# Expert rows gathered whole, against rows gathered as a first half and a second half by index, with part of the second halves left out

## The reference, cut to what matters

```python
u = jnp.take(expert_u, eidx, axis=0)
h = jax.nn.gelu(jnp.einsum('thkd,td->thk', u, xb))
vv = jnp.take(expert_v, eidx, axis=0)
return jnp.einsum('thk,thkd->td', (g * h.astype(jnp.float32)).astype(xb.dtype), vv)
```

## Time and profile before

| | |
|---|---|
| median of three runs | 3214.01 us |
| the three runs | 3214.01, 3211.82, 3215.86 us |
| profiled execution: span from the first to the last instruction | 3210.9 us |
| busy: PE, DVE, ACT, POOL | 79%, 49%, 33%, 18% |
| moved | 1067.8 MB, mean 333 GB/s |

### The profile page before, as it was taken

One profiled execution on the slowest core, in us unless ns is written; L12 is line 12 of the kernel. 1 busy time (PEld: TensorE's weight loads), 2 busy tenths in 40 slices (PEclk: granted clock), 3 DMA queues, 4 the chain that ended last, 5 costly groups with the idle time before them and its releaser, 6 DMA issues.

```text
span 3210.9 us, 43682 instructions
## 1 busy us (share of the span) xinstructions
PE 2530.9 (79%) x17242; PEld 1248.3 (39%) x17242; DVE 1564.1 (49%) x3391; ACT 1048.7 (33%) x2457; POOL 581.5 (18%) x535
## 2 busy tenths in 40 slices
PE   8999988797988878878879878897778655555655
PEld 6677774484322222222228634343324211111111
DVE  4655655763100100100107466678675777777764
ACT  2533443521000000000006354577344444343433
POOL 0000000000000000000000143344443444444442
PEclk9999998998999999999999989898888777788778
DMA  4211302249999999999995499999999999999997
GB/s 152 101 58 66 122 26 112 92 158 382 427 427 427 427 427 427 427 427 427 427 411 195 176 418 399 417 418 383 420 419 420 420 420 419 420 419 420 420 419 331
DMA packets 128670, 1067.80 MB, mean 333 GB/s; under 512 B 14289, under 2 KB 17233, under 8 KB 27601
## 3 DMA queue, kind: packets, MB, share of 16 engines
q0 software_dynamic: 75456, 543.20, 41.0%
q1 hardware_dynamic: 53008, 521.81, 39.4%
HBM read 1051.58 MB, written 13.37 MB: 332 GB/s over the span
## 4 chain that ended last, share of the span: by engine, by line
DMA 50%; PE 34%; DVE 7%; ACT 6%; issue 2%; POOL 1%; ACTq 0%; DVEq 0%; SPq 0%; POOLq 0%
PE ps L92 33%; DMA gb<-in_peer_uv,eidx 27%; DMA gw<-in_eu 14%; DMA gw<-in_ed 8%; DVE gb L146 2%; PE ps L97 2%; ACT L168 1%; ACT dots L168 1%; ACT diag L168 1%; ACT prob L168 1%; POOL gb L86 1%; DVE prob L146 0%; DVE w_lo L115 0%; ACT prob_t L168 0%; DVE prob L120 0%
## 5 line engine op out<-in xcount | busy, mean ns | idle before, releaser
L92 PE MATMUL ps<-gb,diag 64*64 64x512 f32 x4096 | 662.0, 759 | 410.3 <-ACT diag L168 396.8
L146 DVE CUSTOM_DVE_ANT_0 gb<-gb,xn 128x1024 f32<-128x1024 f32 x512 | 627.1, 1225 | 378.5 <-DMA gb<-in_peer_uv,eidx 378.0
L86 POOL DMA_INDIRECT gb<-in_peer_uv,eidx x512 | 570.3, 1114 | 1312.6 <-PE ps L92 718.5
L92 PEld LDWEIGHTS ps<-gb,diag 64*64 64x64 f32 x4096 | 148.2, 155 | 847.6 <-ACT diag L168 746.3
L168 ACT ACTIVATE dots<-dots 128x1 f32<-128x1 f32 (+1 forms) x382 | 77.6, 203 | 618.3 <-DVE dots L146 611.5
L115 DVE TENSOR_TENSOR expert_act<-expert_act,ps 128x512 f32<-128x512 f32 x32 | 22.0, 687 | 523.8 <-PE ps L92 523.2
L92 PE MATMUL ps<-ga,xt 128*64 128x512 f32 x1024 | 229.2, 596 | 41.3 <-DMA ga<-in_eu 32.6
L92 PE MATMUL ps<-gw,xt 128*64 128x512 f32 x992 | 224.3, 601 | 25.4 <-DMA gw<-in_eu 16.2
L168 ACT ACTIVATE diag<-cons,dots 128x128 f32<-128x128 f32 x512 | 205.5, 401 | 41.1 <-ACT dots L168 0.4
L115 DVE TENSOR_TENSOR x<-x,ps 128x512 f32<-128x512 f32 (+1 forms) x96 | 61.4, 643 | 296.5 <-PE ps L92 294.9
L168 ACT ACT_TABLE_LOAD x124 | 159.1, 1283 | 8.1 <-PEq L3241 0.7
(11 more groups left out here) (360 smaller groups left out, 3616.9 us busy)
## 6 DMA issues: line engine op xcount, KB each, us to landing
ga<-in_eu SPq DMA_DIRECT2D x47, 2048.0 KB, 35.5
gw<-in_eg SPq DMA_DIRECT2D x46, 2048.0 KB, 30.7
ring<-in_wt SPq DMA_DIRECT2D x75, 1024.0 KB, 6.0
gw<-in_ed SPq DMA_DIRECT2D x32, 2048.0 KB, 35.5
ga<-in_ed SPq DMA_DIRECT2D x32, 2048.0 KB, 36.1
ga<-in_eg SPq DMA_DIRECT2D x17, 2048.0 KB, 32.2
gw<-in_eu SPq DMA_DIRECT2D x16, 2048.0 KB, 35.5
p_scratch<-spill SPq DMA_DIRECT2D x35, 256.0 KB, 2.1
```

The source lines that it names most:

```text
L86: self.e.indirect_dma_start(out, None, table, bass.IndirectOffsetOnAxis(ap=idx, axis=0)).then_inc(s, 16)
L92: i = self.e.matmul(out, l, r, start=st, stop=sp, skip_group_check=True)
L146: self.done(self.e.tensor_tensor_reduce(out=o, in0=a, in1=b, scale=scale, scalar=start, op0=o0, op1=o1, accum_out=acc), name)
```

## The change

Two views of the same table are used: `peer_uv` as 16384 lines of 8 KB, and `halves`, 32768 lines of 4 KB, in which expert e has its u at 2e and its v at 2e + 1. In each group of four rows (a quad) the first one stays whole, except the first of each block; the other three are fetched in two steps: u at 2e, then, once the four dot products of the quad are there, v at 2e + 1. The index of v gets 65536 added in partitions where the dot product is at or below -11 (`NO_GELU`), where the gelu is exactly zero here; the gather of v has a limit of 32767 on its indices and leaves out those above it, whose partitions then keep what the buffer held, with a weight set to zero. Quads in which a v buffer is used for the first time fetch all of v. Rows 496 to 511 stay whole.

- POOL issues, for each quad g: the four u or whole rows of quad g + 1, then the v of quad g.
- DVE does three more operations of 128x4 for each quad (two `stt` and a `ts`), a doubled index in `dv_choose` in place of a copy, and one more operation on `eidx` a head.
- ACT takes the gelu once for four rows, after DVE's `mask`.
- Sums run up to eight rows behind the dot products. Each buffer of 2048 is used as a u half (free when the dot product is done) and a v half (free after the sum), or for whole rows: 5 pairs and 2 whole from the start, 7 and 3 from row 172, 9 and 4 from row 244.

```diff
+        at = bass.IndirectOffsetOnAxis(ap=idx, axis=0)
+        if last is None:
+            self.e.indirect_dma_start(out, None, table, at).then_inc(s, 16)
+        else:
+            self.e.indirect_dma_start(out, None, table, at, bounds_check=last, oob_is_err=False).then_inc(s, 16)
...
+    NO_GELU, FAR = -11.0, 65536.0
+    halves = I["peer_uv"].rearrange("e (t d) -> (e t) d", t=2)
...
+    def whole(n):
+
+        return n % 4 == 0 and n % 128 != 0 or n >= WHOLE
...
+    U_AT, u_last = places(SPLIT, U_PIECES, "dot")
+    V_AT, v_last = places(SPLIT, V_PIECES, "sum")
+    W_AT, w_last = places([n for n in range(WHOLE) if whole(n)], ROWS_OF, "sum")
...
+    def gated(g):
+
+        return g < WHOLE // 4 and not any(V_AT[n][2] for n in quad(4 * g) if not whole(n))
+
+    def sums_after(n):
+
+        g, j = n // 4, n % 4
...
+        out = []
+        if j == 0 and g >= 1 and whole(4 * g - 4):
+            out.append(4 * g - 4)
+        if j and g >= 2:
+            if j == 1 and not whole(4 * g - 8):
+                out.append(4 * g - 8)
+            out.append(4 * g - 8 + j)
+        return out
...
-            for m in group:
-                yield ("u", m)
-            yield ("w", group)
...
+            yield ("u", n)
+            if n % 4 == 3 or n >= LAST:
+                yield ("k", n)
+            for m in sums_after(n):
+                yield ("w", m)
...
+                pe.wait_ge(("diag", n))
+                if not whole(n):
+                    pe.wait_ge(("v_row", n))
...
+            elif ev[0] == "k":
                 n = ev[1]
...
+                ac.wait_ge(("mask", n // 4) if n < WHOLE else ("dot", n))
+                ac.act(d, d, ACT.Gelu_apprx_tanh, name=("gelu", n))
...
-        dv.cp(sif, siu)
+        dv.ts(sif, siu, 2.0, MUL)
...
+            elif ev[0] == "k" and ev[1] < WHOLE:
+                n = ev[1]
+                i, k = n // 128, n % 128 - 3
+                d, e = dots[:, i % 2, k:k + 4], eidx[i % 2][:, k:k + 4]
+                if gated(n // 4):
+                    s4 = soft[:, i % 2, k:k + 4]
+                    dv.wait_ge(("inv", i, k // 16))
+                    dv.ts(far, d, NO_GELU, ALU.is_le, FAR, MUL)
+                    dv.stt(e, far, 1.0, e, ADD, ADD, name=("v_idx", n // 4))
+                    dv.stt(s4, d, NO_GELU, s4, ALU.is_gt, MUL, name=("mask", n // 4))
+                else:
+                    dv.ts(e, e, 1.0, ADD, name=("v_idx", n // 4))
+                    dv.mark(("mask", n // 4))
...
+        def v_row(n):
+            i, k = n // 128, n % 128
+            s, freed, _ = V_AT[n]
+            po.wait_ge(("v_idx", n // 4))
             if freed is not None:
                 po.wait_ge(freed)
-            po.gather(buf_of(n), I["peer_uv"], eidx[i % 2][:, k:k + 1], f"gb{s}", ("row", n))
+            po.gather(v_of(n), halves, eidx[i % 2][:, k:k + 1], f"gv{s}", ("v_row", n), 2 * 16384 - 1 if gated(n // 4) else None)
+
+        for n in quad(0):
+            u_row(n)
+        for g in range(WHOLE // 4):
+            for n in quad(4 * g + 4):
+                u_row(n)
+            for n in quad(4 * g):
+                if not whole(n):
+                    v_row(n)
+        for n in range(WHOLE + 4, 512):
+            u_row(n)
```

More of the change, by code:

```diff
@@ new lines, in quad, with places @@
+    def quad(n):
+        return range(n - n % 4, n - n % 4 + 4)
+    def places(rows, pieces, end):
+        held, out = [None] * len(pieces), {}
+        for n in rows:
+            s = min((held[s] is not None, rows.index(held[s]) if held[s] is not None else s, s)
+                    for s, (_, first, _) in enumerate(pieces) if n >= first)[2]
+            out[n] = (s, pieces[s][2] if held[s] is None else (end, held[s]), held[s] is None)
+            held[s] = n
+        return out, held
+    SPLIT = [n for n in range(512) if not whole(n)]
@@ L2786, in peer_order @@
+    SUMS = [m for n in range(512) for m in sums_after(n)]
+    assert sorted(SUMS) == list(range(512)) and all(a // 128 <= b // 128 for a, b in zip(SUMS, SUMS[1:]))
+    SUM_AT = {m: q for q, m in enumerate(SUMS)}
+    ROW_ENDS = [SUMS[127], SUMS[255], SUMS[383], LAST - 1]
+    assert SUMS[LAST - 1] == LAST - 1
     def peer_order():
@@ L2791, in peer_order @@
         pass_rows = [24 + 31 * k // 10 for k in range(-1, 52)]
-        n = 0
-        while n < 512:
-            group = row_group(n)
+        for n in range(512):
             ahead = 16 + min(8, n) + max(0, min(8, (n - 8) // 4))
-            need = min(32 * STEPS, STEPS * (ahead + group[-1]) // 16) if n > 2 else STEPS
+            need = min(32 * STEPS, STEPS * (ahead + n) // 16) if n > 2 else STEPS
             while done < need:
@@ L2827, in peer_order @@
                 yield ("q", 1, (n - 194) // 6)
-            n = group[-1] + 1
     def sp_peer(sp):
@@ L2884, in pe_peer @@
+                i, at = n // 128, SUM_AT[n]
+                v, dg = v_of(n), diag[at % 4]
+                if n >= LAST:
+                    if n == LAST:
+                        ends = [few.next() for _ in range(2)]
+                        pe.wait_ge(*ends[0][2], *ends[1][2])
                     pe.wait_ge(("diag", n))
-                    if k == 0:
-                        pe.wait_ge(*left if i == 0 else [("rows_end", i - 1)])
                     for half in range(2):
                         for r in range(2):
[L2889 to L2892, removed]
+                            q = slice(64 * r, 64 * r + 64)
+                            pe.mm(PS[ends[half][0]][q, :], dg[q, q], v[q, 512 * half:512 * half + 512],
+                                  n == LAST, n == 511, ("sum", n) if half and r else ("sum_half", n) if r else None)
+                    continue
@@ new lines, in pe_peer @@
+                pe.wait_ge(("diag", n))
+                if not whole(n):
+                    pe.wait_ge(("v_row", n))
+                if at % 128 == 0:
+                    pe.wait_ge(*left if i == 0 else [("rows_end", i - 1)])
+                for half in range(2):
+                    for r in range(2):
+                        to = r if half == 0 else 1 - r
+                        pe.mm(PS[VB[half]][64 * to:64 * to + 64, :], dg[64 * r:64 * r + 64, 64 * r:64 * r + 64],
+                              v[64 * r:64 * r + 64, 512 * half:512 * half + 512], at % 128 == 0, n == ROW_ENDS[i],
+                              ("sum", n) if half and r else None)
@@ L2937, in ac_peer @@
                     soft_of(ac, i, h)
-            elif ev[0] == "u":
+            elif ev[0] == "k":
                 n = ev[1]
[L2940 to L2945, removed]
-            elif ev[0] == "w":
[L2947 to L2954, removed]
+                first = n if n >= LAST else n - 3
+                i, k = first // 128, first % 128
+                d = dots[:, i % 2, k:k + n - first + 1]
+                ac.wait_ge(("mask", n // 4) if n < WHOLE else ("dot", n))
+                ac.act(d, d, ACT.Gelu_apprx_tanh, name=("gelu", n))
+            elif ev[0] == "w":
+                n = ev[1]
+                i, k, at = n // 128, n % 128, SUM_AT[n]
+                d = dots[:, i % 2, k:k + 1]
+                ac.wait_ge(("inv", i, k // 16))
+                if n < WHOLE:
+                    ac.wait_ge(("mask", n // 4))
+                ac.act(d, d, ACT.Copy, scale=soft[:, i % 2, k:k + 1], name=("weight", n))
+                if at >= 4:
+                    ac.wait_ge(("sum", SUMS[at - 4]))
+                ac.act(diag[at % 4], ident, ACT.Copy, scale=d, name=("diag", n))
             elif ev[0] == "out":
                 i = ev[1]
-                ac.wait_ge(("sum", min(128 * i + 127, LAST - 1)), ("dot", 128 * min(i, 2) + 127))
+                ac.wait_ge(("sum", ROW_ENDS[i]), ("dot", 128 * min(i, 2) + 127))
                 if i == 3:
@@ L3009, in dv_choose @@
         yield
-        dv.stt(eidx[i % 2][:, 16 * h:16 * h + 16], e12[:, 0, :], 128.0, e12[:, 1, :], MUL, ADD, name=("eidx", i, h))
+        dv.stt(eidx[i % 2][:, 16 * h:16 * h + 16], e12[:, 0, :], 128.0, e12[:, 1, :], MUL, ADD)
+        w_ = eidx[i % 2][:, 16 * h:16 * h + 16]
+        if (i, h) != (3, 7):
+            w_ = w_[:, 0 if h else 4:16:4]
+        was, dv.link = dv.link, None if dv.link is None else dv.n
+        dv.ts(w_, w_, 0.5, MUL, name=("eidx", i, h))
+        dv.link = was
         yield
@@ L3057, in po_peer, with u_row @@
     def po_peer(po):
-        for n in range(512):
+        def u_row(n):
             i, k = n // 128, n % 128
-            s, freed = ROW_SLOTS[n]
             po.wait_ge(("eidx", i, k // 16))
+            at = eidx[i % 2][:, k:k + 1]
+            if n >= WHOLE:
+                t, sem, freed = tail_at(n)
+                po.wait_ge(freed)
+                po.gather(t, I["peer_uv"], at, sem, ("row", n))
+            elif whole(n):
+                s, freed, _ = W_AT[n]
+                if freed is not None:
+                    po.wait_ge(freed)
+                po.gather(ROWS_OF[s][0], I["peer_uv"], at, f"gw{s}", ("row", n))
```

(12 more changed lines are left out.)

69 lines of the change are left out of this document (45 added, 24 removed).

## The result

Before 3214.18 us median of four runs, after 3379.91 us (3368.89 to 3386.21, four runs): a ratio of 1.0512, 95% interval 1.0489 to 1.0535. The change makes the kernel 5% slower, where 2.2% faster was forecast. The profiled execution took 3368.89 us with a span of 3367.1, 156.2 above the span of before; it is the fastest of the four, so what follows tells 156 us where the medians differ by 166.

The account below looks back on a forecast made before the run. POOL's gather issues were taken to become the limit in place of bytes: rows 0 to 243 -44, 244 to 495 -12, end -21, start +7, together -70 us. That gave 3140 us of span, 3143 us median; range 3060 to 3245.

Parts of the forecast that it names:

- the loop through POOL: Round from a quad's mask through v and u gathers back to it; 10.8 us a quad early, adding 34 us.
- rival 3: Early loop costs 12 us a quad, DMA engines idle while POOL waits for PE: 3195 us; chance 10%.
- about +65: Upper bound of the change in time, taken with the early loop at 12 us a quad; the fast bound was -174.
- rival 2: POOL's issues fall into step with DVE's dot products, 10.7 us a quad: 3243 us; chance 25%.
- What POOL pays: POOL issues 872 gathers instead of 496, at 1.425 us early and 1.39 late: 10.0 and 9.7 us a quad.
- the price of parity: Issues starting at random meet a running dot product in half the cases and wait 0.25 us on average.
- the late round: Late loop of v, u, dot products and mask takes 17.1 us for two quads, less than 2 x 9.7: hidden.
- The DMA floor: 158 half rows saved, 161 ns a packet; DMA work falls to about 1212 us, -174 if nothing else binds.
- rival 4: The index limit leaves nothing out, or a skipped pick costs as long as a copied one: 3240 us; chance 3%.
- Rival 1: DMA stays the limit, POOL's stalls shrink or limited gathers issue cheaply: 3040 to 3100 us; chance 17%.
- The -21: Gain at the end: sixteen whole rows and a short queue, 40 + 5.5 us where it was 40 + 26.6.
- DVE's added operations: Three small operations add 0.6 us a quad, 7.5 in all, beneath POOL's 9.7: free while POOL binds.

Follow-up runs that it names:

- six_v_pieces: The changed kernel with a fifth early u piece turned into a sixth v piece; 3296.94 us, ratio 1.0258.
- split_from_176: The changed kernel with rows 0 to 175 fetched whole and summed at once, two-step fetching from row 176; 3253.67 us, ratio 1.0114.
- from_176_lead: split_from_176 with, from quad 62 on, u of quad g + 2 issued ahead of v of g; 3241.69 us, ratio 1.0075.
- from_176_psum: split_from_176 with dot products from row 256 on reading the normed token from PSUM; 3195.83 us, ratio 0.9938.
- xn_in_psum: The changed kernel with dot products from row 256 on reading the normed token from PSUM; 3369.35 us, ratio 1.0478.
- no_limit: The changed kernel with every v fetched in all 128 partitions, no index limit and no mask; 3363.44 us, ratio 1.0461.
- psum alone: Only the token read from PSUM from row 256 on: 3369.35 us on the changed kernel, 3195.83 us on split_from_176.
- all_from_0_lead_psum: The changed kernel, split from row 0, with token in PSUM from row 256 and u two quads ahead from quad 62; 3279.61 us, ratio 1.0199.
- from_176_lead_psum: split_from_176 with both token in PSUM from row 256 and u two quads ahead from quad 62; 3154.96 us, ratio 0.9813.

## Why the prediction was wrong, point by point

**The step that failed is "the loop through POOL", and in it the early quads.** I took 10.8 us a quad, with 12 as the bad end; it was 14.6. That alone is 43 x 3.8 = 164 of the 227 us between 3140 and 3367. Its terms: landing was taken at 5.5, the shortest of 1816 to 2506 us, where the median was 14.1; by the updates of the gathers' semaphores in the trace of after it is, in the median, 7.6 for u and 6.4 for v in rows 0 to 171, 6.9 and 5.9 in rows 244 to 495. Dot product and mask were taken at 1.9, as if one row were late; four landed rows stand in line on DVE, with choosing steps between, 6.5 us (2920.0 to 2926.5 in the trace of after), though part of that passes while the last of them is still in flight. And the third v went out 14.3 us after the start of the last dot product, not 6.0: by the kernel's order the sum it waits for stands behind this quad's gelu and whatever PE and ACT have in hand of the mixing layer (how much each of them costs no run tells apart). Over quads 20 to 41 (those that meet the start of a block left out) the round has, in the mean, 13.7 us to the third v, 5.7 to the last u, 7.9 for its landing and 2.5 to the start of its dot product: 29.9 for two quads, where 18.6 was reckoned, 24 with all that might stand in its way. I had the mechanism (rival 3) and priced it as a sum of shortest durations, so its 12 wasn't a bound. six_v_pieces and split_from_176 show it. (Nor does the "about +65" of the sum follow from its own terms: rival 2 and the loop at 12 together are -70 + 100 + 52 = +82.)

**"What POOL pays" was right in kind, short in size.** POOL became the limit late (gaps of 0.30, from_176_lead), at 1.48 us an issue and not 1.39: 7 x 0.09 x 63 = 40 us, more than the 35 by which rows 244 to 495 missed. The mean that I took came from issues spread out by waits for PE; of those that follow one another at once, the kernel before already shows 1.43 us from 2506 to 3175 (60 of them) and 1.49 over the whole stage (174). The stall of the earlier trace rows ended 0.81 us after the dot product did, as all others; the forecast read 0.89, from the start of the record behind it. I had written that starts at random would meet a dot product in half the cases and called it "the price of parity". That is what happened: 197 of 392. Rival 2's in-step pattern wasn't needed. It said that it decides from 1.49.

**A second limit stood close behind it.** I called the late round hidden, 17.1 against 2 x 9.7. It holds 2 x 9.66 when the issues aren't held up (from_176_psum), longer than 17.1 for the two sizes named above, and loosening it takes the quads on to 8.98. In after POOL limits and the round is close: from_176_lead gains only 12 us. The 10 us of xn_in_psum it doesn't explain; see "Open".

**The DMA floor was right in its parts.** 158 half rows, 76,048 packets of 4 KB for the layer forecast as about 76,000, 159 ns for 161. The 9.0 us a quad was reached as 8.98 with the DMA engines full, though POOL's own sum there is 8.96, so the agreement is in part luck. A pick left out still leaves a packet: 20,208 of 4 bytes beyond the sixteen of that size that every gather has, 9 ns each, in 4 KB packets' place. The limit itself adds 0.05 us to an issue (shortest 985 for 932 ns), so "costs like any other" held and rival 4 is out. Rival 1 is out too.

**The end gained nothing.** The -21 counted a queue of 26.6 us as gone at the end; counted by dot products that queue was filled in the early rows, and the last sixteen rows took 40.0 us for 38.3.

**DVE's added operations** at nothing: no run takes them out alone. Late DVE is busy 69%, and no_limit, which has fewer of them, is only 16 us below after, so there is little room for them.

**Signs.** Gaps, packets and landing under 12 us came as written; POOL early half busy, 333 to 340 GB/s for 370 and DVE's wait for rows did not (436 us for 378 before). The mean issue is 1.15 over the stage, just inside, and 1.18 late. The stage took 1538 us from first issue to last landing, for 1315. "Rival 3 as POOL waiting for PE in the first 43 quads with a DMA share under 0.9" is, word for word, what the trace shows.

**Open:** why psum alone gained 10 us on the changed kernel and 58 us on the one split from row 176, both with the same order of late gathers. all_from_0_lead_psum excludes carried-over work only where the round is loosened; the round of two quads settled at 21.0 us in one and 19.3 in the other. The waits of ACT and PE from 2750 to 3100 us differ (first xn_in_psum, then from_176_psum; L172 writes the diagonals, "remote" is a releaser that the profile can't name, "issue" idle time for which it shows no wait):

```profile
ACT diag L172 <- remote: 128.2, 26, 9.9
...
PE ps L96 <- issue: 85.7, 30, 9.0
```

```profile
ACT dots L172 <- DVE soft L130: 187.2, 36, 9.1
...
PE ps L96 <- ACT diag L172: 140.6, 36, 9.0
```

In the second ACT waits for the mask and PE for ACT, as in after. In the first ACT waits ahead of its diagonals; the diagonal of a quad's second row comes 19.6 us after the quad's last dot product has started, for 14.1 (means of quads 75 to 117), and POOL waits for sums ahead of its v. So it is the sums that come late there. What keeps PE from them no run tells.

## What to carry to other kernels

Before counting on bytes saved, price each loop that the change closes through an in-order queue with the durations that its members have in a line (four dot products, not one; landing under load, not the shortest), and put what may wait last in the queue or give it one more buffer. Read the price of a resource that is about to become the limit from back-to-back uses in the old trace, not from its mean. When an experiment that removes a proven limit gains nothing, look for a second one close behind it before dropping the theory: here one fix alone gave 12 us, the other 58, and both gave 99. And the length of a loop over two quads, taken from the trace, is twice the pace whatever limits; to see whether the loop limits, look for a pause in the queue that it goes through.

## What the runs showed of the hardware that I had not expected

A gather's issue that begins during a dot product with both operands in SBUF is held for the rest of it, and ends 0.81 us after it, 0.87 with the limit (1.38 us against 0.98 in the mean). It is only the beginning that is held. Of the issues of before from 2506 to 3100 us, 54 had a dot product begin more than 0.13 us after their own start, and they took 938 ns in the mean, where the shortest of all is 932. The issue at 2922.39 shown above was held until 2923.31 and then ended in 0.83 us, although the next dot product had begun at 2923.57. With one operand in PSUM the hold is gone: 0.991 us for issues that begin during a dot product, 0.987 for the others (224 and 234 of them in from_176_lead_psum). The Trainium skill, SBUF — State Buffer, "Who interferes with whom", says that an elementwise operation of two tensors with both inputs in SBUF contends with GpSimd's reads, which agrees, as the gather takes its indices from SBUF. It also infers that descriptor generation is free of it; the 0.81 us that run on beside the next dot product don't speak against that, though no run here tells which part of an issue writes descriptors. The hold is one operation's rest, never the 3100 ns that the forecast cited: the longest issue of the gathers in the kernel after is 2.05 us.

A DMA share of 0.93 to 0.94 left room for 17% more rows a second: packets were longer while the queue was short (177 ns in the mean, 159 in the median), so the share doesn't say how much more fits. That the short queue is the reason is argued from the traces alone: with landings of 6.7 us in the median (after, 2600 to 3000 us) the mean packet took 178 ns, with 7.9 us (from_176_lead_psum) 165.
